# Last squares of the gate stage summed by single-column matmuls, first half chunk of weights rounded on VectorE

## What is computed

```python
def rms_norm(x, gain, eps=EPS):
    xf = x.astype(jnp.float32)
    y = xf * lax.rsqrt(jnp.mean(xf * xf, axis=-1, keepdims=True) + eps)
    return (y * gain.astype(jnp.float32)).astype(x.dtype)
...
        h = rms_norm(x, pre_norm_gain[i])
        proj = h @ w_in[i]
...
        e = rms_norm(p[i] @ w_ple_proj[i], ple_norm_gain[i])
        x = x + jax.nn.sigmoid(x @ w_ple_gate[i]) * e
...
def fourier_mixer(h, w_o):
    B, S, D = h.shape
    hg = h.astype(jnp.float32).reshape(B, S, FOURIER_GROUPS, FOURIER_GROUP_DIM)
    f = jnp.fft.fftn(hg, axes=(1, 3), norm="ortho").real.astype(h.dtype)
    return f.reshape(B, S, D) @ w_o
...
        h = modulate(rmsnorm(x, norm_mix_g[i]), sh1, sc1)
        m = fourier_mixer(h, w_fourier_out[j])
```

## Time and profile before

| what | us |
|---|---|
| median of 3 runs | 1549.35 (1549.2 to 1550.66) |
| the profiled execution, its own time | 1549.36 |
| its span, first to last instruction | 1547.2 |
| PE busy in the span | 1534.6 (99%) |
| DVE, ACT, POOL busy | 797.9, 599.1, 868.8 |

### The profile page before, as it was taken

How to read it: one execution, slowest core, us unless ns; L and a number is a source line. 1 busy time by engine, 2 the same in 40 slices (tenths; PEclk the granted TensorE clock), 3 DMA queues, 4 the chain that set the end, 5 groups by cost and what they waited for, 6 DMA issues and landing times.

```text
span 1547.2 us, 21282 instructions
## 1 busy us (share of the span) xinstructions
PE 1534.6 (99%) x7254; PEld 1274.5 (82%) x7254; DVE 797.9 (52%) x1127; ACT 599.1 (39%) x886; POOL 868.8 (56%) x1040
## 2 busy tenths in 40 slices
PE   9999999999999999999999999999999999999997
PEld 7777878898888888888888888888889888888886
DVE  6887887887645544551555424346257454011113
ACT  6444444584522212223444334244345322122223
POOL 6445548657577755775464535535535766555551
PEclk9999999999999999999999999999999999999999
DMA  6534455234355554542221322312212553222221
GB/s 230 193 127 158 165 212 194 84 135 164 110 189 200 194 190 177 207 150 99 100 98 68 110 78 83 105 41 107 95 54 82 204 204 122 96 95 95 95 82 55
DMA packets 58250, 202.97 MB, mean 131 GB/s; under 512 B 6481, under 2 KB 8529, under 8 KB 58193
## 3 DMA queue, kind: packets, MB, share of 16 engines
q1 hardware_dynamic: 56896, 198.87, 36.2%
q10 hardware_dynamic: 1296, 3.30, 0.6%
HBM read 200.05 MB, written 2.10 MB: 131 GB/s over the span
## 4 chain that ended last, share of the span: by engine, by line
PE 77%; POOL 11%; issue 10%; ACT 1%; DVE 1%; DMA 0%; POOLq 0%; DVEq 0%; ACTq 0%
PE banks L1724 21%; PE banks L1727 21%; PE banks L1728 21%; POOL w_lo L413 11%; PE banks L2229 2%; PE banks L2230 2%; PE banks L2226 2%; PE banks L1740 1%; PE banks L1743 1%; PE banks L1744 1%; PE banks L2265 1%; PE banks L2266 1%; PE banks L2264 1%; PE banks L2252 0%; PE banks L2253 0%
## 5 line engine op out<-in xcount | busy, mean ns | idle before, releaser
L413 POOL TENSOR_TENSOR w_lo<-w_raw,w_hi 128x256 fp32r<-128x256 f32 x1028 | 861.6, 871 | 643.4 <-ACT w_hi L445 643.4
L445 ACT ACTIVATE w_hi<-w_raw 128x1024 fp32r<-128x1024 f32 x257 | 270.2, 1057 | 641.8 <-PE banks L1724 582.7
L1724 PE MATMUL banks<-a_hi,w_lo 128*128 128x512 f32 x1228 | 482.0, 393 | 0.2 <-POOL w_lo L413 0.2
L1728 PE MATMUL banks<-a_hi,w_hi 128*128 128x512 f32 x1228 | 478.2, 389 | 0.0
L1727 PE MATMUL banks<-a_lo,w_hi 128*128 128x512 f32 x1228 | 478.0, 389 | 0.0
L1724 PEld LDWEIGHTS banks<-a_hi,w_lo 128*128 128x128 f32 x1228 | 230.8, 188 | 48.3 <-issue 0.8
L1728 PEld LDWEIGHTS banks<-a_hi,w_hi 128*128 128x128 f32 x1228 | 230.5, 188 | 48.2
L1727 PEld LDWEIGHTS banks<-a_lo,w_hi 128*128 128x128 f32 x1228 | 230.6, 188 | 47.0 <-issue 0.2
L1724 PE MATMUL banks<-b_hi,w_lo 128*128 128x512 f32 x572 | 223.5, 391 | 0.1
L1727 PE MATMUL banks<-b_lo,w_hi 128*128 128x512 f32 x572 | 222.6, 389 | 0.0
L1728 PE MATMUL banks<-b_hi,w_hi 128*128 128x512 f32 x572 | 222.6, 389 | 0.0
(11 more groups left out here) (289 smaller groups left out, 1641.3 us busy)
## 6 DMA issues: line engine op xcount, KB each, us to landing
w_raw<-in_W SPq DMA_DIRECT2D x258, 512.0 KB, 3.5
ada_raw<-in_ADA SPq DMA_DIRECT2D x112, 512.0 KB, 4.3
X<-in_XT SPq DMA_DIRECT2D x8, 256.0 KB, 6.4
scr<-in_DECAY ACTq DMA_DIRECT2D x4, 448.0 KB, 3.8
out<-X SPq DMA_DIRECT2D x5, 256.0 KB, 2.5
w_raw<-in_W SPq DMA_DIRECT2D x2, 256.0 KB, 4.1
scr<-in_PT ACTq DMA_DIRECT2D x1, 512.0 KB, 4.8
scr<-in_ROPE ACTq DMA_DIRECT2D x1, 512.0 KB, 4.5
```

Of the source, the lines that this page charges most:

```text
L413: pool.tensor_tensor(w_lo[:, c % RING, part], w_raw[:, c % RING, part], w_hi[:, c % RING, part].bitcast(fp32), ALU.subtract).then_inc(wlo, 1)
L445: act.activation(w_hi[:, c % RING, :], w_raw[:, c % RING, :], ACT.Copy).then_inc(whi, 1)
L1724: mm = pe.matmul(out, lo, x_hi, start=first, stop=False)
L1728: mm = pe.matmul(out, hi, x_hi, start=False, stop=last)
```

## The change

Two edits, which are independent of each other.

First, the gate stage. A constant OWN = 5 splits the eight squared tiles. Tiles 0 to 4 are summed by VectorE as before. Tiles 5 to 7 are squared by ACT into `E[:, m, :]` in SBUF (the slot of the embedding tile that has just been used up), not into a bank, and VectorE's three additions for them are gone. `rinv_columns` now runs, for each block of 128 tokens, one single-column matmul over `sqsum` and three over `E`, added up in the same column of `aux`. The banks of gate tiles 5 to 7 are now freed by ACT's `XH` instruction of that tile.

Second, the start. VectorE rounds the first half chunk (a new `tensor_copy` ahead of its first `a_lo`, semaphore `start_hi`), ACT goes from `a_hi` of tile 0 directly to the second half. TensorE takes k = 1 in groups of four matmuls too: high-high, then `w_lo`, then `a_lo`. WARM is not changed.

```diff
@@ scalar, start
             def halves(c):
-                act.activation(w_hi[:, c, 0:HT * 2], w_raw[:, c, 0:HT * 2], ACT.Copy).then_inc(first_hi, 1)
+                if c:
+                    act.activation(w_hi[:, c, 0:HT * 2], w_raw[:, c, 0:HT * 2], ACT.Copy).then_inc(first_hi, 1)
...
                 if m == 0:
-                    act.wait_ge(first_in, 16)
                     halves(0)
@@ scalar, gate_post
-                dst = banks[:, BANK[t0 + m], :] if m else sqsum[:, :]
+                dst = sqsum[:, :] if m == 0 else banks[:, BANK[t0 + m], :] if m < OWN else E[:, m, :]
...
-                if m:
+                if 0 < m < OWN:
                     ins.then_inc(xh, 1)
                 else:
-                    read_out(ins, t0)
+                    read_out(ins, t0 + m)
@@ vector, start
+            dve.wait_ge(first_in, 16)
+            dve.tensor_copy(w_hi[:, 0, 0:HT * 2], w_raw[:, 0, 0:HT * 2]).then_inc(start_hi, 1)
             for m in range(KD):
                 raw_low(m)
@@ vector, gate
-                if m > 1:
+                if 1 < m <= OWN:
                     add_gate_square(m - 1)
                 if m:
                     xg_low(m - 1)
-            add_gate_square(KD - 1)
             xg_low(KD - 1)
@@ tensor, gemm with norm
-                    pe.wait_ge(first_hi, 1)
-                    pe.wait_ge(h_hi, KD * norm + 1)
...
+                    for n, k in enumerate(ks[0:2]):
+                        if n == 0:
+                            pe.wait_ge(start_hi, 1)
+                        else:
+                            pe.wait_ge(whi, 1)
+                        pe.wait_ge(h_hi, KD * norm + n + 1)
...
@@ tensor
             def rinv_columns():
-                wait_read(pe, flat, TI["gate"] + KD - 1)
+                wait_read(pe, flat, TI["gate"] + OWN - 1)
+                pe.wait_ge(sq_ready, 8 * 3 + KD)
                 pe.wait_ge(aux_free, AUX["four"])
                 for tt in range(TB):
-                    mm = pe.matmul(aux[:, tt:tt + 1], sqsum[:, tt * P:(tt + 1) * P], ones[:, 0:1], start=True, stop=True)
+                    tokens = slice(tt * P, (tt + 1) * P)
+                    pe.matmul(aux[:, tt:tt + 1], sqsum[:, tokens], ones[:, 0:1], start=True, stop=False)
+                    for m in range(OWN, KD):
+                        mm = pe.matmul(aux[:, tt:tt + 1], E[:, m, tokens], ones[:, 0:1], start=False, stop=m == KD - 1)
                 mm.then_inc(aux_ready, 1)
```

More of the change, by code:

```diff
@@ L39 @@
 ADA_LAG = 6
+OWN = 5
 COL = {}
@@ L238, in build @@
         x_in = [sem(f"x_in{m}") for m in range(KD)]
-        first_in, first_hi, rest_in = sem("first_in"), sem("first_hi"), sem("rest_in")
+        first_in, first_hi, rest_in, start_hi = sem("first_in"), sem("first_hi"), sem("rest_in"), sem("start_hi")
         cols_in, p_in, dist_in, rope_in, dec_in = (
@@ L418, in _ @@
                     if q % 2 == 0:
-                        pool.wait_ge(whi if q else first_hi, c + 1)
+                        pool.wait_ge(*((whi, c + 1) if q else (first_hi if c else start_hi, 1)))
                     part = slice(q * QW, (q + 1) * QW)
@@ L1354, in xg_low @@
             def xg_low(m):
-                if m:
+                if 0 < m < OWN:
                     dve.wait_ge(xh, m)
                 else:
-                    wait_read(dve, flat, t0)
+                    wait_read(dve, flat, t0 + m)
                 dve.scalar_tensor_tensor(out=XL[:, m, :], in0=X[:, m, :], scalar=gs[:, KD + m:KD + m + 1],
@@ L1835, in gemm @@
                 if norm is not None:
-                    pe.wait_ge(first_hi, 1)
-                    pe.wait_ge(h_hi, KD * norm + 1)
[L1838 to L1851, removed]
+                    for n, k in enumerate(ks[0:2]):
[4 more added lines that the diff above has]
+                        pe.wait_ge(h_hi, KD * norm + n + 1)
+                        x_hi, x_lo = rhs(k)
+                        weights = [chunk_begins(at, P, waits=False) for m in range(4)]
+                        for m, (_, hi, lo) in enumerate(weights):
+                            pe.matmul(banks[:, BANK[t0 + m], :], hi, x_hi, start=n == 0, stop=False)
+                            opened.add(m)
+                            n_of[m] = n + 1
+                        if n == 0:
+                            ready(k)
+                            for m, (_, hi, lo) in enumerate(weights):
+                                pe.matmul(banks[:, BANK[t0 + m], :], hi, x_lo, start=False, stop=False)
+                        for m, (_, hi, lo) in enumerate(weights):
+                            if m % 2 == 0:
+                                pe.wait_ge(wlo, 2 * n + m // 2 + 1)
+                            mm = pe.matmul(banks[:, BANK[t0 + m], :], lo, x_hi, start=False, stop=False)
+                        if n == 1:
+                            ready(k)
+                            for m, (_, hi, lo) in enumerate(weights):
+                                pe.matmul(banks[:, BANK[t0 + m], :], hi, x_lo, start=False, stop=False)
+                        seen.add(k)
@@ L1852, in gemm @@
                 for n, (k, m) in enumerate(order):
-                    if norm is not None and n < 4:
+                    if norm is not None and n < 8:
                         continue
```

## The result

The changed kernel takes 1553.22 us in the median (1551.54 to 1555.7, 11 runs); the kernel before, measured beside it, 1549.27 us (1548.93 to 1550.66, 11 runs). The ratio is 1.0024, 95% interval 1.0017 to 1.0032. I had forecast 1550.9 with a range up to 1552.6, so the time is outside it. It is 0.3 us from the rival in which TensorE's clock falls (1553.5), to which I had given 7 in 100.

A forecast was written before the change was run, and what follows sets the result against it. TensorE's own stream was taken to bound the kernel. Removed waits -1.05, added columns +2.67 and start -0.05 summed to +1.57 on 1549.36, so 1550.9 us, 0.10% slower; the range was 1549.0 to 1552.6, without the clock case.

The forecast's parts named there:

- the rival in which TensorE's clock falls: Behind the gate's column block, TensorE drops to half rate: 2.5 us lost, +4.1 in total, 1553.5 us; chance 0.07.
- What bounds the kernel: Whole kernel: TensorE, busy 1534.6 of 1547.2 us; edits count only by work or waits in its own stream.
- The price of the columns: Column block between g = 2 and g = 3: 24 more records at 0.111 each, 2.67 us more on TensorE.
- the rival of cheap columns: Column block: a single-column record costs only 0.03, so the change gives -0.4, or 1549.0 us; chance 0.05.
- The waits taken out: Gate group g = 2: two TensorE waits on VectorE's additions go, so the columns start 1.05 us earlier, bounds 0.5 and 1.15.
- The wait for gate tile 6's bank: Middle of g = 2: ACT's `XH` frees the bank at 324.63, needed at 325.45, so the wait goes.
- The wait for `XL` of tile 5: Start of g = 2: `XL` ends at 323.92 and releases at 323.97, ahead of the stream at 324.01; the wait goes.
- my lower bound of 0.5: Gate group g = 2: the gain from removed waits if one of the two waits stays, against 1.05 forecast.
- The start: First product: VectorE's copy is ready earlier, but the ones fill TensorE until 6.26; gain -0.05 us, from 0 to -0.25.
- The chain behind the columns: Columns' end to second half of g = 3, over `rcol`, `a_hi`, `a_lo`: 2.76 us without slack, moving later by 1.62.
- so it is near but below: Column block: its 3.5 us stretch stays under the 3.9 us after which the clock fell at the kernel's end.
- it is not empty: Column block: the 3.5 us stretch still holds TensorE work, an argument against the clock falling there.

The follow-up runs named there:

- gate only: The kernel before with OWN = 5 and only the gate's lines of the change, its start unaltered: 1553.63 us, ratio 1.0024 to before.
- 128 columns: The changed kernel with each matmul of the column block streaming 128 columns of ones instead of one: 1551.45 us, repeated 1551.65, before 1549.53 and 1549.69.
- columns left out: The changed kernel without the twelve added column matmuls, so squares of tiles 5 to 7 are not summed: 1549.43 us, ratio 0.9999 to before.
- changed kernel again: The changed kernel unaltered, run once more beside the kernel before on one chip: 1554.31 us against 1549.69, ratio 1.0031.
- OWN = 6: The changed kernel with OWN = 6 instead of 5, so tiles 6 and 7 are summed by single columns: 1552.69 us, ratio 1.0016 to before.
- OWN = 7: The changed kernel with OWN = 7 instead of 5, so only the last squared tile is summed by single columns: 1549.89 us, ratio 1.0001 to before.
- start-only: The changed kernel with only the start edit kept, its squares and four column matmuls those of before: 1549.33 us, ratio 0.9997 to before.
- broken up: The changed kernel with six unused matmuls of 256 columns between the second and third token block of the columns: 1554.52 us, ratio 1.0028 to before.
- late additions: The changed kernel with VectorE adding tiles 5 to 7 late from SBUF and one column matmul per token block: 1551.51 us, ratio 1.0010 to before.
- unused matmuls in the wait: VectorE adding tiles 5 to 7 late, plus eight unused 256-column matmuls where TensorE waits for the last addition: 1549.48 us, ratio 1.0000 to before.

## Why the prediction was wrong, point by point

**What bounds the kernel.** Right. TensorE's stream sets the time; VectorE's freed 1.8 us bought only a part of what TensorE waited for.

**The price of the columns.** Right: 24 records more, 2.67 forecast, 3.49 - 0.81 = 2.68 measured. The page's floor of 25 ns (the Trainium skill, "TensorE: Matmul & The Clock Gate", "Back-to-back issue gap") plays no part at this shape, and the rival of cheap columns is out.

**The waits taken out.** Half right. The wait for gate tile 6's bank went. The wait for `XL` of tile 5 did not: 1.05 was forecast, 0.55 measured, which is near my lower bound of 0.5. The step that failed is "now it ends at 323.92, just ahead of the stream". VectorE's timeline of the changed kernel:

```profile
322.81 1.30 DVE L1362 SCALAR_TENSOR_TENSOR b_lo<-X,gs,b_hi 128x512 fp32r<-128x512 f32 x1
```

It begins 0.96 earlier than before (323.77 in the earlier trace rows) but takes 1.30 in place of 0.75, and ends at 324.11. With 0.75 it would have ended at 323.56, ahead of the 323.66 at which the stream gets there. This is so in the traces of four more kernels with OWN = 5 (gate only, 128 columns, columns left out, changed kernel again), and not with OWN = 6 or 7, where an addition still stands ahead of it and it takes 0.75. The order before also had one of 1.28, so the operation has two durations. What stands beside it is GpSimd's `w_lo` subtraction. After the change:

```profile
322.82 0.74 POOL L414 TENSOR_TENSOR w_lo<-w_raw,w_hi 128x256 fp32r<-128x256 f32 x1
323.52 1.19 POOL L414 TENSOR_TENSOR w_lo<-w_raw,w_hi 128x256 fp32r<-128x256 f32 x1
```

And before:

```profile
323.18 0.74 POOL L413 TENSOR_TENSOR w_lo<-w_raw,w_hi 128x256 fp32r<-128x256 f32 x1
323.88 1.23 POOL L413 TENSOR_TENSOR w_lo<-w_raw,w_hi 128x256 fp32r<-128x256 f32 x1
```

After the change the operation begins together with a piece of GpSimd's (322.81 and 322.82), and takes 1.30, about as long as if it waited for most of that piece and then ran its 0.75. Before, it began when a piece was nearly done (323.77, with an end at 323.92), took 0.75 itself, and GpSimd's next piece took 1.23 in place of 0.74. The earlier slow one fits as well: 315.46 on VectorE, 315.45 on GpSimd. The thirteen traces agree without an exception: of all `XL` operations, the 22 that begin within 0.02 us of the start of a piece take 1.27 to 1.31, one that begins 0.08 behind it takes 1.21, and all others take 0.74 or 0.75. So the two seem to run one after the other, and the addition taken out moved `XL` of tile 5 onto the start of a GpSimd piece. My sum had no term for GpSimd. No run moved GpSimd's work, so this is read from the traces and not tested. That the stream was 0.35 early is not the reason: in the gate-only trace it is 0.36 late and waits as long, 0.34.

**The start.** Right in kind and size, 0.05 forecast and 0.03 in the trace of the start alone. In the start-only trace, whose ones take 5.06 as before, PE's first product is recorded at 6.13 behind 22 records of ones, and VectorE's copy was done long before:

```profile
1.42 5.06 PE L1928 MATMUL banks<-ones_r 128*128 128x128 f32 x22 [1.42 <-DVE ones_r L1130]
6.13 1.40 PE L1848 MATMUL banks<-a_hi,w_hi 128*128 128x512 f32 x4
...
5.21 0.43 DVE L1148 CAST w_hi<-w_raw 128x512 fp32r<-128x512 f32 x1 [3.23 <-DMA w_raw<-in_W]
```

The copy took 0.43, under my 0.49 to 0.61. What I had not seen is that a start can be earlier by more, and that most of it can be given back. In the changed kernel's profiled execution the clock rose sooner: 22 records of ones in 4.12 us, first product at 5.48, and the stream was 1.1 us ahead of before at 30 us. Near 55 us TensorE then waits for VectorE's low part of the attention weights, where it did not wait before, and is 0.33 ahead behind that:

```profile
1.41 4.12 PE L1927 MATMUL banks<-ones_r 128*128 128x128 f32 x22 [1.41 <-DVE ones_r L1130]
5.48 1.20 PE L1847 MATMUL banks<-a_hi,w_hi 128*128 128x512 f32 x4
...
55.12 0.66 PE L1954 MATMUL banks<-cols,scr 128*128 128x128 f32 x4 [0.59 <-DVE b_lo L1206]
```

It need not be given back: in the trace with the added columns left out the ones took 4.12 too, and the stream still was 0.8 ahead at 320 us. Nor does the edit alone bring it: the start-only trace has the ones at 5.06 with the same edit.

**The chain behind the columns.** I had it as a rigid 2.76 with a last wait of 0.6. From 330.63 to 333.40 it is 2.77, so its length was right. The wait shrank to 0.24, because the matmuls inside the 2.77 had already become slower.

**The clock.** This is the step that made the prediction wrong. The mechanism and the place stood in the rival, and nearly the price: 2.5 us for a fall was forecast, 2.19 measured, and 3.97 in sum against 4.1. That the price came so close is in part luck. I took 5.1 us at half rate, half of it lost; it was 6.8 us, but the first 1.35 of them (332.05 to 333.40) lie inside the chain behind the columns and cost nothing, behind that a matmul is 0.21 from the next in place of 0.12, and 0.23 comes back at a gap ahead of 337.36 that the slower stream no longer has. What failed is its chance of 0.07, and with it the upper end of the range. I had argued from one row: at the kernel's end the clock fell 3.9 us after the last matmul, the new stretch is 3.5 us, "so it is near but below". The runs show four faults in that. The stretch does not end with the block: a fall came with 2.6 us of columns, with 3.5 us that were broken up, and with a wait of 0.9 and eight records behind it. The 3.9 us ran from the last matmul to the fall, but here the fall came 1.4 us behind the end of the block (1.5 behind that of the late additions), in a dense stream, so the two lengths could not be compared. And one instance of an event that varies from one execution to the next is no threshold: even the changed kernel was without a fall in 3 of 19. Last, "it is not empty" was wishful, since the loads of weights in it did not keep the clock up. The Trainium skill's rule ("TensorE: Matmul & The Clock Gate", Part 1, "What's actually happening") is about how busy TensorE has been. The profile shows TensorE busy for all of the block (3.50 of 3.50 us between 327 and 330.5) and the clock fell; with 128 columns streamed by the same records it did not. Had this rival not been left out of the range, its upper end would have been 1553.5, which holds the time. Without a fall the forecast was some 0.4 too low, near the 0.5 by which the waits were overrated: with 128 streamed columns, where the block is as long and the clock stays up, the kernel is 1.9 to 2.0 us above before in the median, against +1.57.

## What to carry to other kernels

When an edit moves an operation in time, look also at what the other engines do at its new place: here VectorE's `XL` of tile 5 took 1.30 in place of 0.75 beside GpSimd.

Before putting small matmuls or a wait on TensorE into an otherwise dense stream, look at what it streams around that place as well as at how busy it is shown, and give the clock's fall a real chance; its price here was about 2 us each time it happened. Where it threatens, try a wider moving operand (128 columns cost nothing more than one here) or unused matmuls in the wait. Both took the fall away in these runs; neither made the kernel faster than before. A matmul with one column and 128 stationary ones costs 0.22 us in fp32 for its two records, so additions are given to TensorE cheaply only where it stands still anyway, and there too the clock has to be watched, as the late additions showed.

## What the runs showed of the hardware

A record of an fp32 matmul with a full 128-column stationary operand takes 0.11 us whether 1 or 128 columns are streamed. Where the clock fell behind the columns, the granted clock was at 1.2 GHz for 6.8 us in five traces and for 3.4 us in one, although the stream was dense again. The fall began 1.4 us behind the block in the changed kernel's trace. VectorE's `XL` operation (two inputs and an output in SBUF, 128x512) took 1.30 when it began together with a GpSimd subtraction of 128x256, and 0.75 when it began near the end of one, with the next subtraction at 1.23 in place of 0.74. At the kernel's start the ones ran at half rate, and in the traces the clock rose at different moments: 22 records of ones took 4.12 and 4.37 us in the two traces of the changed kernel, and 5.06 in others with the same start. What exactly decides a fall stays open: it came in no execution with OWN = 7, in 7 of 11 with OWN = 6, and in 16 of 19 of the changed kernel, so it also varies from one execution of the same program to the next.
